# One SBUF layout for the whole program, and the second table's transfers issued by ScalarE

## The reference, cut to what matters

```python
def mixer(xn, ...):
    glu, qkv, b_raw, a_raw, z, gates = jnp.split(xn @ w_in, pts, axis=-1)
    c_in = glu[..., :CONV_DIM] * jax.nn.sigmoid(glu[..., CONV_DIM:])
    c, conv_new = causal_dwconv(c_in, conv_prev, conv_dw_w)
    c = jax.nn.silu(layer_norm(c + conv_dw_b, conv_ln_g, conv_ln_b))
    y_conv = c @ conv_pw2
    qkv, dconv_new = causal_dwconv(qkv, dconv_prev, dn_conv_w)
    ...
    o, s_new = gated_delta_chunked(q, k, v, beta, g, s_prev, chunk)
    o = o * lax.rsqrt(jnp.mean(o * o, -1, keepdims=True) + EPS) * dn_norm_g
    y_dn = (o * jax.nn.silu(z)) @ dn_w_o
    g_conv, g_dn = jnp.split(jax.nn.sigmoid(gates), 2, axis=-1)
    return (g_conv * y_conv + g_dn * y_dn) @ w_out, ...

def peer(xn, w_q, sub_keys, u, v):      # 16384 experts of one neuron, 8 heads, top 16
    q = (x2 @ w_q).reshape(n, PEER_HEADS, 2, PEER_HALF)
    s = jnp.einsum('nhpd,hpkd->nhpk', q, sub_keys)
    ...                                  # top 16 of both halves, top 16 of their sums, softmax
    hid = jnp.einsum('pd,phkd->phk', xb, u[ib])
    act = jax.nn.gelu(hid) * gb
    return jnp.einsum('phk,phkd->pd', act, v[ib])
```

## Time and profile before

| | us |
|---|---|
| median of 3 runs | 5441.45 |
| lowest, highest | 5441.27, 5454.98 |
| profiled execution | 5447.09 |
| its span, first to last instruction | 5445.5 |
| TensorE busy (matmuls) | 5096.0 (94%) |
| VectorE busy | 3004.9 (55%) |
| ScalarE, GpSimd busy | 865.0, 886.4 (16% each) |
| mean granted TensorE clock | 0.972 |
| moved by DMA | 1083.10 MB |

### The profile page before, as it was taken

How to read it: one execution, slowest core, us unless ns; L and a number is a source line. 1 busy time by engine, 2 the same in 40 slices (tenths; PEclk the granted TensorE clock), 3 DMA queues, 4 the chain that set the end, 5 groups by cost and what they waited for, 6 DMA issues and landing times. The chain is left out here.

```text
span 5445.5 us, 70952 instructions
## 1 busy us (share of the span) xinstructions
PE 5096.0 (94%) x23085; PEld 3818.8 (70%) x23085; DVE 3004.9 (55%) x3912; ACT 865.0 (16%) x1388; POOL 886.4 (16%) x760
## 2 busy tenths in 40 slices
PE   7999998999999799989845999999999999999996
PEld 5555555877777577977635777777777777777774
DVE  1465653333332111027865777776777777777776
ACT  1111112111110000111166111111111111111110
POOL 0000000000000001310000333333422333333321
PEclk8999999999999899999978999999999999999998
DMA  2111111111121423131189988988999998989996
GB/s 103 66 64 58 64 52 70 55 52 52 55 85 50 175 100 135 69 124 62 39 140 199 357 336 343 348 336 332 351 352 349 347 346 340 341 337 345 346 350 234
DMA packets 339220, 1083.10 MB, mean 199 GB/s; under 512 B 154208, under 2 KB 175072, under 8 KB 253152
## 3 DMA queue, kind: packets, MB, share of 16 engines
q1 hardware_dynamic: 264288, 541.95, 28.9%
q0 software_dynamic: 74752, 538.99, 26.0%
HBM read 1014.60 MB, written 66.25 MB: 198 GB/s over the span
## 5 line engine op out<-in xcount | busy, mean ns | idle before, releaser
L1706 PE MATMUL ps<-aT,work 128*128 128x384 f32 x4096 | 1373.2, 488 | 28.1 <-DVE aT L1815 24.6
L1706 PEld LDWEIGHTS ps<-aT,work 128*128 128x128 f32 x4096 | 775.6, 191 | 514.3 <-issue 44.9
L1690 PE MATMUL ps<-xhi,whi 128*128 128x384 f32 x2048 | 758.7, 370 | 27.5 <-ACT whi L1751 27.5
L411 PE MATMUL ps<-arena 128*128 128x320 f32 x2560 | 714.1, 434 | 1.8 <-issue 1.3
L1691 PE MATMUL ps<-xlo,whi 128*128 128x384 f32 x2048 | 685.8, 335 | 0.0
L365 PE MATMUL ps<-arena 128*128 128x512 f32 x1280 | 656.5, 595 | 7.7 <-DVEq L776 7.7
L1809 DVE TENSOR_TENSOR wlo<-work,whi 128x1024 fp32r<-128x1024 f32 x256 | 313.6, 1225 | 609.6 <-ACT whi L1751 547.1
L1895 POOL DMA_INDIRECT work<-in_peer_u,cur_u x256 | 416.8, 1628 | 1280.7 <-DVE hid L1842 1270.6
L411 PEld LDWEIGHTS ps<-arena 128*128 128x128 f32 x2560 | 478.7, 191 | 191.9 <-issue 10.9
L1852 DVE SCALAR_TENSOR_TENSOR rows<-work,act_w,rows 128x2048 f32<-128x2048 f32 x256 | 600.4, 2345 | 1.1 <-DMA work<-in_peer_v,cur_v 0.5
L1751 ACT ACTIVATE whi<-work 128x1024 fp32r<-128x1024 f32 x256 | 271.5, 1060 | 2065.9 <-DMA work<-in_u_units 2043.6
(11 more groups left out here) (276 smaller groups left out, 4569.0 us busy)
## 6 DMA issues: line engine op xcount, KB each, us to landing
work<-in_u_units SPq DMA_DIRECT2D x256, 512.0 KB, 8.4
work<-in_v_units SPq DMA_DIRECT2D x256, 512.0 KB, 6.8
d_ring<-in_w_units SPq DMA_DIRECT2D x48, 1024.0 KB, 4.8
arena<-in_w_group SPq DMA_DIRECT2D x40, 1024.0 KB, 4.8
arena<-in_w_units SPq DMA_DIRECT2D x40, 1024.0 KB, 5.0
gates_dram<-work SPq DMA_DIRECT2D x8, 3072.0 KB, 21.1
gbuf<-gates_dram SPq DMA_DIRECT2D x128, 192.0 KB, 7.6
gates_T<-arena SPq DMA_DIRECT2D x40, 320.0 KB, 2.4
```

The lines of the kernel that those rows point to most:

```text
L411: m = pe.matmul(ps[0][:, half * 512:half * 512 + HT], homes[r][:, k, :], xnT[:, k, half * HT:half * HT + HT], start=k == 0, stop=k == KD - 1)
L1690: pe.matmul(out, h3[:, k, :], xhi[:, 8 * half + k, :], start=half == 0 and k == 0, stop=False)
L1706: mmi = pe.matmul(out, w4[:, q, e, :], aT[:, (1 - par) * ET + e, :], start=e == 0, stop=e == ET - 1)
```

## The change

The SBUF array is split in two. `keep` (20480 columns) holds `cT`, `qT`, `vT` and `kT` and lives through all three blocks; the rest stays in `arena`.

- First block: `cT_spill` and `oT_spill` are gone. The z rows are written by ScalarE into `vT`'s place (`zT`), no longer to HBM. The `z_w` buffers move into `kT`'s place, so their first loads wait until the streams' tile has copied k, q and v (`dd["copied"]`). In that tile the first 22 gate steps (12 and 10) move to its end (62 becomes 84), and ScalarE's halves are dealt out anew. The last two calls of `load_z` fetch the first two units of the second block.
- Second block: `cz`, `of`, `zf` are `cT`, `qT`, `zT` as they stand, and `ring` is `z_w`'s place. No load stands before the merge. `xT_spill` and `sel_spill` are gone; `sel` is written in place; `xhi` and `xlo` are made here, between the transposes and the queries, after `xg_spill` has left the place they take.
- Third block: it starts with the transposes of `sel`. ScalarE issues the loads of the second table, each after its wait on `v_mm`, ahead of that step's `whi`.

```diff
-        XNT, CT, QT, KT, VT, WR, TM = 0, 10240, 15360, 20480, 25600, 30720, 40960
+        CT, QT, VT, KT, XNT, WR, TM = 0, 5120, 10240, 15360, 20480, 30720, 40960
-        z_w = [at(CT + i * D, KD, P) for i in range(2)]
-        gate_out, z_out = at(WR + 1024, T), at(CT + 2 * D, T)
+        z_w = [at(KT + i * D, KD, P) for i in range(2)]
+        gate_out, late_out = at(WR + 1024, T), at(KT + 2 * D, T)
+        zT = at(VT, H, T)
 ...
-            sp.wait_ge(ln_out, NC)
-            sp.dma_start(cT_spill, cT).then_inc(spilled, 16)
 ...
             sp.dma_start(state_new_p, at(WR, H * P)).then_inc(st_out, 16)
-
+            sp.wait_ge(dd["copied"], PT + 1)
+            load_z(GWR)
+            load_z(GWR + 1)
 ...
             for n in range(GWR, NG):
                 sp.wait_ge(gate_act, 2 * n + 2)
-                store(n, z_out)
-                if n + 2 < NG:
-                    load_z(n + 2)
+                if n < 2 * KD:
+                    store(n, late_out)
+                load_z(n + 2)
 
             sp.wait_ge(dd["snew"], PT * 2 + 2 * H)
             sp.dma_start(state_new_s, st_s_dst).then_inc(st_out, 16)
             sp.wait_ge(st_out, 32)
-            sp.wait_ge(dd["out"], TILES)
-            sp.dma_start(oT_spill, qT).then_inc(spilled, 16)
 ...
-                gates(12)
+                gates(0 if streams else 12)
 ...
-                gates(10)
+                gates(0 if streams else 10)
 ...
-                    gates(62)
+                    gates(84)
 ...
-            load(0, 0)
-            load_pieces(sp, cz, cT_spill, c_in)
-            for k in range(4):
-                sp.dma_start(piece(of, k), piece(oT_spill, k)).then_inc(o_in[k], 16)
-                sp.dma_start(piece(zf, k), gates_T[2 * KD + 2 * k:2 * KD + 2 * k + 2].rearrange("a p n -> p a n")).then_inc(z_in[k], 16)
-            load(1, 1)
 ...
-            sp.wait_ge(n_evac, 2 * TILES)
-            sp.dma_start(xT_spill[:, :, 0:TD], x2[:, :, 0:TD]).then_inc(spill_done, 16)
 ...
+            sp.wait_ge(spill_done, 16)
             sp.wait_ge(selected, 1)
-            sp.dma_start(sel_spill, selbuf).then_inc(spill_done, 16)
-            sp.wait_ge(spill_done, 48)
 ...
+            act.wait_ge(spill_done, 16)
+            for k in range(4):
+                act.activation(piece(xhi, k), piece(x2, k)[:, :, 0:TD], ACT.Copy).then_inc(xhi_done, 1)
 ...
+            for k in range(4):
+                v.wait_ge(xhi_done, k + 1)
+                v.tensor_tensor(piece(xlo, k), piece(x2, k)[:, :, 0:TD], piece(xhi, k).bitcast(F32), ALU.subtract).then_inc(xsplit, 1)
 ...
-            sp.dma_start(sel[:], sel_spill).then_inc(sel_ld, 16)
-            load_pieces(sp, xT, xT_spill[:, :, 0:TD], xT_ld)
-
-            sp.wait_ge(xsplit, 4)
             sp.dma_start(rows2[:, 0:GT * D], x1_spill[:, DT * D:]).then_inc(rows_ld, 16)
 ...
-                    if has_v:
-                        wait_count(sp, "sp", v_mm, c * (2 * NU) + (2 * j + 2 - 2 * NU))
-                        sp.dma_start(vraw[j % 2], v_units[bass.ds(c * NU + (j - NU), 1)].rearrange("a p n -> p (a n)")).then_inc(vn_ld[j % 2], 16)
 ...
+                    if has_v:
+                        wait_count(act, "act", v_mm, c * (2 * NU) + (2 * j + 2 - 2 * NU))
+                        act.dma_start(vraw[j % 2], v_units[bass.ds(c * NU + (j - NU), 1)].rearrange("a p n -> p (a n)")).then_inc(vn_ld[j % 2], 16)
```

More of the change, by code:

```diff
@@ L104, in build @@
         par = ctx.enter_context(nc.sbuf_tensor("par", [P, PW], F32))
+        with ExitStack() as later:
+            xhi, xlo = (later.enter_context(nc.sbuf_tensor(n, [P, KD, TD], F32R)) for n in ("xhi", "xlo"))
+        KEEP = 20480
+        keep = ctx.enter_context(nc.sbuf_tensor("keep", [P, KEEP], F32))
         ps = [ctx.enter_context(nc.psum_tensor(f"ps{i}", [P, 1024], F32)) for i in range(4)]
-        XNT, CT, QT, KT, VT, WR, TM = 0, 10240, 15360, 20480, 25600, 30720, 40960
+        CT, QT, VT, KT, XNT, WR, TM = 0, 5120, 10240, 15360, 20480, 30720, 40960
         END = 49152
-        arena = sb("arena", [P, END])
+        arena = sb("arena", [P, END - KEEP])
         def at(off, *dims):
@@ L638, in halves @@
                         n, half = pos[0] // 2, pos[0] % 2
[L639 to L643, removed]
+                        late = type(base) is int and base + n >= GWR
+                        out, func = late_out if late else gate_out, ACT.Sigmoid
+                        if late and base + n >= 2 * KD:
+                            out, func = zT[:, base + n - 2 * KD, :], ACT.Silu
                         w(gate_mm, base * 2 + (pos[0] + 1))
-                        if half == 0 and not (first and base + n == 0):
+                        if half == 0 and func is ACT.Sigmoid and not (type(base) is int and base + n == 0):
                             w(gate_st, base * 16 + 16 * n)
@@ L681, in delta @@
                 act.activation(vc, vT[:, :, tile], ACT.Copy).then_inc(dd["copied"], 1)
-                gate(1)
+                gate(0 if streams else 1)
                 w(dd["gexp_in"], tot(1, 1))
@@ L693, in delta @@
                 act.activation(eb, eb, ACT.Exp).then_inc(dd["eexp"], 1)
-                gate(3)
+                gate(2 if streams else 3)
                 for l in range(lev):
@@ L702, in delta @@
                         act.activation(xb[:, 4 * g:4 * g + 4, :], ps8(1)[:, 4 * g:4 * g + 4, :], ACT.Copy).then_inc(dd["xc"], 1)
[L703 removed]
+                    if l in ((0, 2, 3) if streams else (1, 3, 4, 6)):
                         gate(1)
                 if streams:
[L706 removed]
+                    gate(1)
                     act.wait_ge(dd["ksT"], 2)
@@ L1781, in _ @@
             v.wait_ge(sel_cp, 3)
-            split_lo(v, xT, xhi, xlo, xhi_done, xsplit)
             v.wait_ge(iota_ready, 2)
```

100 lines of the change are left out of this document (35 added, 65 removed).

## The result

The changed kernel takes **5399.93 us** (median; 5398.74 to 5403.35) beside 5442.34 for the kernel before on the same chip: ratio 0.9918, 95% interval 0.9901 to 0.9935, 42.4 us less. In two of the experiments one run lies far outside the others (11150.33 us in e9, 6773.29 in e10); the medians given include it.

What follows compares the result with a forecast made beforehand. TensorE was taken to bound the third block's steps, with gains only where it waited at block starts. Terms 0 - 8.9 - 16.0 + 1.0 = -23.9 us took 5441.45 to 5417.6 us; range 5404 to 5440.

Steps and rivals of the forecast that it cites:

- Part 1: First block, streams' tile: 22 gate steps move to its end, so the last gate comes 6.0 us later.
- Part 2: First block's end: the dropped store pays for the moved gate steps; 0 us, between -1.5 and +1.4.
- Part 3: Second block's start: TensorE starts with VectorE, first merge unit done sooner; -8.9 us, between -6.8 and -11.0.
- Part 4: Second block, expert rows: `xhi` and `xlo` are made while VectorE sat idle; 0 us, about 9 without that cover.
- Part 5: Third block's start: no store and load before the transposes, one-hot rows sooner; -16.0 us, between -14 and -17.
- Part 6: Third block's steps: ScalarE issues the v loads; only the first v unit loses, +1 us, between 0 and 2.
- Rival C: Third block's steps: freed u loads go out earlier and TensorE's 24.6 us of waits halve; -12 us, 5405; chance 0.12.
- Rivals A and B: Chunk loop's turns: a third busy queue stretches VectorE's waits; 5438 (chance 0.17), or slower than before, 5480 if doubled (0.10).

Runs made afterwards that it cites:

- e9: Changed kernel with an extra v_mm wait ahead of the third unit's u load only, and that load halved: 5398.95 us.
- e10: Changed kernel with extra v_mm waits ahead of all overlapping u loads but the third unit's, one row gather in 16 cut to 16 of 128 rows: 5438.84 us.
- e6: Changed kernel with the first block's states' store issued four gates before the last: 5396.95 us.
- e11: Changed kernel with the first block's states' store issued right behind the last z unit's load: 5390.57 us.
- e2: Kernel before, old layout, with only the v unit loads moved to ScalarE's queue: 5418.87 us.
- e4: Kernel before, one queue, with each u load issued one place earlier, ahead of the v_mm wait and v load: 5417.32 us.
- e13: Changed kernel plus a 2.6 MB DRAM-to-DRAM copy by SyncE once in two chunks, some 3 us ahead of VectorE's turn: 5459.01 us.
- e12: Kernel before, with one row gather in 16 cut to 16 of 128 rows: 5435.66 us.
- e8: Changed kernel with an extra v_mm wait ahead of every u load that overlaps the v part except the third unit's: 5440.87 us.
- e3: Changed kernel, two queues kept, with SyncE's u loads held back behind a v_mm wait as before: 5433.21 us.
- e7: Changed kernel with an extra v_mm wait ahead of the third unit's u load only: 5399.72 us.

## Why the prediction was wrong, point by point

- **Part 1**, the last gate 6.0 us later: 6.45. The path was right, the cover's size not: TensorE waited 4.76 us for the copies (until 1580.05), and the small products behind them took 7.5 us and not 5.7, the first four alone 3.78.
- **Part 2**, 0 us: +3.4. This term was mis-sized. The load of 1 MB ahead of the store in its queue was charged with a quarter of the store's time, 2.9 us at most. The store landed 16.1 us after its issue, about the store's old 11.5 and the load's 4.8. The load itself landed after 6.7 us, so the two shared the DMA engines, and here the transfer ahead counted in full. e6 and e11 show the store to be the cause of 11.5 us of the gap.
- **Part 3**, -8.9 us: -5.2, and the difference is part 2's. From the block's first instruction to the finished unit 19.3 us were forecast and 19.7 measured.
- **Part 4**, 0 us: nothing on TensorE's path waits there for the expert rows.
- **Part 5**, -16.0 us: -16.9 (22.1 less 5.2). 2.5 us of it are lost again up to the first u matmul; the forecast handed all of it on.
- **Part 6**, +1 us: -28.6. This is the step that failed. Of the second queue it said the right thing, that it is worth nothing; e2 and e4 show it, 1.6 us apart. The +1 was meant for the first v part, and there TensorE waited 4.10 us for `aT` and 1.7 for a v unit, where before it had waited 2.33. But it costed the move only for the instruction that moved (does the v load still arrive?) and never for those that it was **moved away from**. SyncE's u load had stood behind that wait, and the row that shows it was there: `whi <-DMA work<-in_u_units` in the earlier trace rows, 7.04 us in a single step. The part's closing argument, that v and u units landed well ahead of their use, misread it: ScalarE waited for the data of 246 u units, 1995 us in all.

  What the runs showed in its place: the u loads, freed from that wait, end the late row work and gathers (this link is argued, see below), VectorE's turns fall from 3.6 to 6.4 us to 3.4 to 3.6, and TensorE loses 20.5 us less in waits for `aT` and some 7 less to the clock behind them (9.6 against 2.8, by the estimate above), 27 of the 28.6.
- **Rival C** named the mechanism, with less than half its size and 0.12 of the chance. Its "against" was a wrong argument: what follows the turn needs no u unit, true, but the turn itself gets longer by what late u units push to it. It treated the 5.2 us of a turn as a constant of the machine, though the earlier trace rows has it between 5.2 on average and 6.4 at most, and a duration that varies has a cause.
- **Rivals A and B** had the right sensitive place, the turns, and the right lever, transfers in flight. They ran the wrong way, since with the same bytes moved the turns became shorter; e13, which adds 2.6 MB at each turn, shows what a grown backlog costs (+59 us).
- The sum: forecast -24.9 at the first u matmul and -23.9 at the end; measured -19.6 and -48.3.

What stays open: which transfers, and how many bytes, hold the instruction packet back. Two turns of before took 3.6 us with the DMA engines at 0.9 to 1.1 throughout, and one of e4 took 5.6 us with 0.9 at its start, where another with 0.8 took 3.4. e10 took 0.9 MB away without effect where e12 took the same away and gained 8 us (13 in the steps of the profiled runs). Why e8 is slower than e3 is not known. That late row work and gathers are the link between late u units and long turns follows from the order of events in e7 and e8; e12 supports it in part, and no run moved the gathers alone.

## What to carry to other kernels

When a wait or a transfer leaves an engine's queue, cost what stood **behind** it there as carefully as the thing itself: here the v loads could go to any queue or stay, and all of the gain in the steps lay in the u loads that no longer stood behind their wait. In this loop, with the DMA engines busy 0.9 of the time, what decided was how busy they were when VectorE turned; loads issued as early as their buffers allowed left a lull there. The large store at the block's end did best right behind the last load that the block itself still needed: 9.4 us below after by medians, where two loads earlier it gained 3.0.

## What the runs showed of the hardware

- A turn of VectorE's loop is no constant: 3.4 to 3.6 us in after, 5.7 to 7.1 with a 2.6 MB copy issued some 3 us ahead of it. In all 159 turns traced a packet on the instruction queue ends 1.2 to 1.9 us before VectorE goes on, and the turn is long where that packet starts late (from 0.5 to 5.5 us into the turn).
- A wait of TensorE can cost more than its length, but need not. Behind the 2.95 us wait at 3162 the granted clock was 0.50 to 0.56 for 3 us (1.2 GHz) and ten matmuls took 5.15 us and not 3.46. In before this followed 4 of the 12 waits (of 2.33, 2.95, 2.94 and 2.14 us); behind the other eight, of 0.4 to 2.4 us, the ten took 3.46. In e13 it followed the waits at all eleven turns traced (2.3 to 3.6 us).
- Block to block, 9 us passed from the last landing to the next block's first instruction, in four kernels; TensorE stood still for 13.5 us where a 1 MB load was the last to land and 25.0 where a 4 MB store was.
